# A two-layer streaming encoder on one Trainium2 core: single-group dense turns, residual adds and squares on GpSimd, and two rounds of picks in a step

## The reference, cut to what matters

```
xn  = rmsnorm(x, norm1)                       # x * rsqrt(mean(x*x) + eps) * gain
u   = xn @ w_in                               # one projection, 4292 columns, cut among three mixers
oa  = differential attention (6 heads)        # softmax over two maps, block-causal
ob  = sparse attention (5 heads)              # an indexer scores the keys,
      _, sel = lax.top_k(score, n_sel)        # 256 of them are kept per query (136 for the sample)
oc  = HGRN2 linear recurrence (5 heads)
x   = x + concat(oa', ob, oc') @ w_out
a, gate = split(rmsnorm(x, norm2) @ w_up)     # 2 x 2816 columns
x   = x + (silu(causal_conv3(a)) * gate) @ w_down
```

## Time and profile before

| | us |
|---|---|
| median of 3 runs | 4510.31 (4510.25 to 4512.2) |
| the profiled execution | 4511.78 |
| its span, first to last instruction | 4510.0 |
| TensorE busy | 4080.2 (90%) |
| VectorE busy | 2281.9 (51%) |
| ScalarE busy | 996.6 (22%) |
| GpSimd busy | 224.3 (5%) |
| mean granted TensorE clock | 0.919 of 2.4 GHz |

### The profile page before, as it was taken

How to read it: one execution, slowest core, us unless ns; L and a number is a source line. 1 busy time by engine, 2 the same in 40 slices (tenths; PEclk the granted TensorE clock), 3 DMA queues, 4 the chain that set the end, 5 groups by cost and what they waited for, 6 DMA issues and landing times.

```text
span 4510.0 us, 47853 instructions
## 1 busy us (share of the span) xinstructions
PE 4080.2 (90%) x19244; PEld 2705.0 (60%) x19244; DVE 2281.9 (51%) x4647; ACT 996.6 (22%) x2287; POOL 224.3 (5%) x172
## 2 busy tenths in 40 slices
PE   7888788998889999998999998997899998899998
PEld 6665446776767767773444444486767776644443
DVE  1833454597942454439635555298924555522222
ACT  1113222110113333221223222011123332210001
POOL 2200220000000003100000000400000000000000
PEclk9995788999999999899998989998999998899999
DMA  3321122211120212221221211331121111122222
GB/s 127 109 91 31 53 64 90 77 66 47 52 84 18 69 61 73 87 84 70 70 74 49 73 56 55 108 110 56 45 79 54 47 55 56 37 85 65 77 75 73
DMA packets 142165, 310.33 MB, mean 69 GB/s; under 512 B 29160, under 2 KB 69608, under 8 KB 130680
## 3 DMA queue, kind: packets, MB, share of 16 engines
q1 hardware_dynamic: 81432, 262.25, 17.7%
q10 hardware_dynamic: 60512, 45.02, 3.5%
HBM read 271.08 MB, written 36.14 MB: 68 GB/s over the span
## 4 chain that ended last, share of the span: by engine, by line
PE 73%; DVE 19%; ACT 3%; issue 2%; DMA 1%; ACTq 1%; SPq 0%; DVEq 0%
PE PS L600 49%; PE PS L607 6%; DVE scr L1227 5%; DVE top L1226 5%; PE PS L698 4%; PE PS L687 3%; PE PS L671 3%; PE PS L657 2%; PE PS L576 2%; PE PS L794 1%; PE PS L725 1%; PE PS L793 1%; DVE inv L1164 1%; ACT scr L989 1%; DVE xn L1167 1%
## 5 line engine op out<-in xcount | busy, mean ns | idle before, releaser
L600 PE MATMUL PS<-xn,wring 128*128 128x272 f32 (+1 forms) x6048 | 1906.8, 477 | 74.1 <-DVE xn L1167 48.6
L600 PEld LDWEIGHTS PS<-xn,wring 128*128 128x128 f32 x6048 | 1188.2, 198 | 748.1 <-issue 552.6
L600 PE MATMUL PS<-dense,wring 128*128 128x272 f32 (+1 forms) x2112 | 681.3, 482 | 55.3 <-DVE xT L1173 45.9
L600 PEld LDWEIGHTS PS<-dense,wring 128*128 128x128 f32 x2112 | 417.2, 201 | 288.2 <-issue 217.2
L1173 DVE TENSOR_TENSOR xT<-PS,xT 128x272 f32<-128x272 f32 (+1 forms) x240 | 123.4, 523 | 499.0 <-PE PS L600 497.9
L1226 DVE MAX8 top<-scr 128x8 f32<-128x384 f32 (+6 forms) x418 | 367.5, 879 | 12.7
L1227 DVE MATCH_REPLACE8 scr<-top,scr 128x384 f32<-128x384 f32 (+6 forms) x418 | 359.9, 861 | 0.0
L607 PE MATMUL PS<-wring,xn 128*128 128x224 f32 (+1 forms) x1728 | 350.1, 364 | 10.5 <-ACT dense L865 10.5
L607 PEld LDWEIGHTS PS<-wring,xn 128*128 128x128 f32 (+1 forms) x1728 | 318.0, 187 | 35.5 <-ACT dense L865 11.2
L698 PE MATMUL PS<-kv,scr 128*128 128x64 f32 (+2 forms) x1804 | 249.5, 289 | 14.9 <-ACT scr L989 14.9
L698 PEld LDWEIGHTS PS<-kv,scr 128*128 128x128 f32 (+2 forms) x1804 | 237.6, 202 | 33.8 <-ACT scr L989 21.3
(11 more groups left out here) (160 smaller groups left out, 3090.8 us busy)
## 6 DMA issues: line engine op xcount, KB each, us to landing
wring<-in_wu SPq DMA_DIRECT2D x88, 1024.0 KB, 4.8
wring<-in_wf SPq DMA_DIRECT2D x76, 512.0 KB, 3.3
wring<-in_wd SPq DMA_DIRECT2D x64, 384.0 KB, 3.1
wring<-in_wn SPq DMA_DIRECT2D x24, 896.0 KB, 4.9
wring<-in_wd SPq DMA_DIRECT2D x64, 320.0 KB, 2.9
wring<-in_wo SPq DMA_DIRECT2D x32, 512.0 KB, 3.3
kv<-out_projT ACTq DMA_DIRECT2D x48, 256.0 KB, 4.3
out_projN<-dense SPq DMA_DIRECT2D x96, 112.0 KB, 1.7
```

Source lines behind the costliest of these rows:

```text
L600: mm = nc.tensor.matmul(PS[:, dbank(t.g0 + j), 0:cw], wtile(t.q, i), rhs, start=(kk == a), stop=(kk == b - 1))
```

## The change

- **Turns of one group.** `GRP` of h=1 becomes two groups of 256 columns, and every turn now does a single group j. For f, a, g and the dn of parts 0 to 2 the two groups of a block follow each other; for wo and the last dn all 8 blocks of group 0 come first and then all 8 of group 1 (`_added`), so their weight tiles are loaded twice: 64 more tile loads.
- **Banks of wo and dn are emptied by ScalarE** into one of two buffers `res` (`NRES`), and GpSimd adds that into `xT` (SBUF to SBUF). VectorE's add is gone.
- **Squares of a norm on GpSimd**: in wo turns and in the last dn turns, behind each add, GpSimd squares the block and adds it to a running sum, kept in two blocks of `xn`. The norm's matmul is then one instead of eight, against a matrix of 1/1024 (`mean`). Only the two norms of layer 0's projections still square on ScalarE, into `catT`.
- **Norms by group**: group 0's norm stands behind the third turn of group 1, group 1's behind the first turn of the next stage that uses group 0.
- **Picks**: `BURST = 2`. `weave`'s estimates and leads are adapted; `tout` has two buffers in place of three (`NTO`).
- **Start**: SP loads `mean`, the first half of `xT` (a semaphore per block) and three weight tiles, then the constants and the second half. TensorE waits for `mean` alone.

The core of the diff:

```
-GRP = (((0, 272), (272, 272)), ((0, 512),))
+GRP = (((0, 272), (272, 272)), ((0, 256), (256, 256)))
-BURST = 4
+BURST = 2
...
+def _added(kind, l, h, p, norm):
+    for j in range(2):
+        for n in range(KD):
+            _turn(kind, l, h, n, p, j, load=(kind, l, h, n, p))
+            if (n, j) == (2, 1):
+                _norm(*norm, 0)
 def _ffn(l, h):
-    for n in range(KD):
-        _turn("wo", l, h, n, load=("wo", l, h, n, 0))
-    _norm(l, h, 1)
+    _added("wo", l, h, 0, (l, h, 1))
...
+                order = ("a", 0), ("a", 1), ("g", 0), ("g", 1)
+                for kind, j in (("a", 0), ("g", 0), ("a", 1), ("g", 1)) if n == 0 else order:
+                    _turn(kind, l, h, n, 0, j, load=("u", l, h, n, 0))
+                    if (kind, n, j) == ("a", 0, 0):
+                        _norm(l, h, 1, 1)
...
 dense_scalar:
+                elif t.kind in ("wo", "dn"):
+                    i = ADDS[k]
+                    act.wait_ge(s_res, max(0, i - NRES + 1))
+                    act.wait_ge(s_mm, t.g0 + 1)
+                    nc.scalar.activation(res[:, i % NRES, 0:cw], PS[:, dbank(t.g0), 0:cw], ACT.Copy).then_inc(s_ea, 1)
 dense_vector:
-                elif t.kind in BY_DVE:
-                    for j, (c, cw) in enumerate(GRP[t.h]):
-                        dve.wait_ge(s_mm, t.g0 + j + 1)
-                        x = xT[:, t.n, xcols(t.h, c, cw)]
-                        nc.vector.tensor_tensor(x, PS[:, dbank(t.g0 + j), 0:cw], x, ALU.add).then_inc(s_ed, 1)
 pool_program:
+                if t.kind in ("wo", "dn"):
+                    c, cw = GRP[t.h][t.j]
+                    x, i = xT[:, t.n, xcols(t.h, c, cw)], ADDS[k]
+                    pool.wait_ge(s_ea, t.g0 + 1)
+                    pool.wait_ge(s_xn, KD * norms_before(k))
+                    nc.gpsimd.tensor_tensor(x, x, res[:, i % NRES, 0:cw], ALU.add).then_inc(s_res, 1)
+                    if t.kind == "wo" or t.p == 3:
+                        total, here = xn[:, SUM, c:c + cw], xn[:, SUM + 1, c:c + cw]
+                        pool.wait_ge(s_res, i + 1)
...
+                            own(nc.gpsimd.tensor_tensor(here, x, x, ALU.mult))
+                            ins = nc.gpsimd.tensor_tensor(total, total, here, ALU.add)
...
 sync_program:
+            sp.eng.dma_start(mean[:], io["mean"]).then_inc(s_mean, 16)
             for k in range(KD):
-                sp.eng.dma_start(xT[:, k, :], io["xT"][k * P:(k + 1) * P, :]).then_inc(s_x, 16)
+                sp.eng.dma_start(xT[:, k, 0:W[0]], io["xT"][k * P:(k + 1) * P, 0:W[0]]).then_inc(s_x[0][k], 16)
```

More of the change, by code:

```diff
@@ L282, in weave @@
         l, h = PROJS[m]
-        first = F_TURN[l, h, 5] + 4 if kind == "X" else STAGE["P%d%d" % (l, h)][1] + 3
+        first = LAST["f", l, h, 5, 0] + 1 + LAG if kind == "X" else STAGE["P%d%d" % (l, h)][1] + LAG
         for pe, act, dve, wait in step_times(kind, m):
             steps.append((first, 0.3 + max(wait, act + dve if kind in "CM" else max(act, dve))))
-    turns = [(i, max(0.5, turn_time(TURNS[i])[0])) for i in dense]
+    turns = [(i, turn_time(TURNS[i])) for i in dense]
     have, need = sum(t for i, t in turns), sum(max(0.2, t) for first, t in steps) or 1
@@ L352, in sem @@
             return ctx.enter_context(nc.semaphore(name))
-        ident, ones = sb("ident", [P, P]), sb("ones", [P, P])
+        ident, mean = sb("ident", [P, P]), sb("mean", [P, P])
         lmask, bmask = sb("lmask", [P, NL, 32]), sb("bmask", [P, 4, 32])
@@ L569, in dense_tensor @@
                 if t.kind == "nsq":
-                    N = norm_index(k)
-                    for kk in range(KD):
-                        pe.wait_ge(s_sq, KD * N + kk + 1)
-                        for j, (c, cw) in enumerate(GRP[t.h]):
-                            if kk == 0:
-                                bank_free(pe, t.g0 + j)
-                            mm = nc.tensor.matmul(PS[:, dbank(t.g0 + j), 0:cw], ones[:], sq[:, kk % 2, c:c + cw],
-                                                  start=(kk == 0), stop=(kk == KD - 1))
-                            if kk == KD - 1:
-                                mm.then_inc(s_mm, 1)
-                        if kk < KD - 1:
-                            mm.then_inc(s_sqf, 1)
+                    c, cw = GRP[t.h][t.j]
+                    out = PS[:, dbank(t.g0), 0:cw]
+                    bank_free(pe, t.g0)
+                    if t.p:
+                        for kk in range(KD):
+                            pe.wait_ge(s_sq, KD * norms_before(k) + kk + 1)
+                            mm = nc.tensor.matmul(out, mean[:], catT[:, kk, c:c + cw], start=(kk == 0), stop=(kk == KD - 1))
+                    else:
+                        pe.wait_ge(s_acc, norms_before(k) - 4 + 1)
+                        mm = nc.tensor.matmul(out, mean[:], xn[:, SUM, c:c + cw], start=True, stop=True)
+                    mm.then_inc(s_mm, 1)
                 elif t.kind in ("f", "wo", "a", "g", "dn"):
@@ L635, in idx_tensor @@
                     dots(y, 1)
-                elif what == "pick" and z == 4 and y + 1 < len(PICKS[h]):
+                elif what == "pick" and z == 6 and y + 1 < len(PICKS[h]):
                     dots(y + 1, 0)
@@ L868, in dense_scalar @@
                     U = m * NF + t.n
-                    if t.kind == "a" and t.n == 0:
+                    if t.kind == "a" and t.n == 0 and t.j == 0:
                         for i in range(2):
                             act.wait_ge(s_st[i], max(stored(PROJ_BEFORE[m], r) for r in range(NB) if (PROJ_BEFORE[m] * NB + r) % 2 == i))
-                        for i in range(3):
-                            act.wait_ge(s_to[i], 16 * len([x for x in range(T_COUNT[PROJ_BEFORE[m]]) if x % 3 == i]))
+                        for i in range(NTO):
+                            act.wait_ge(s_to[i], 16 * len([x for x in range(T_COUNT[PROJ_BEFORE[m]]) if x % NTO == i]))
@@ L889, in dense_scalar @@
+                    ins.then_inc(s_ea, 1)
+                    if t.kind == "g" and t.j == 1:
                         pending = (t.l, t.h, t.n, U)
@@ L1151, in dense_vector @@
             for k, t in enumerate(TURNS):
-                if pending is not None and t.kind in ("g", "dn"):
+                if pending is not None and (t.kind == "dn" or k >= LAST[("g",) + pending[0:3] + (0,)] + 2):
                     product()
@@ L1612 @@
         "wd": tiles(a["ffn_down"], P), "rope": np.stack(table(32) + table(64)).transpose(1, 0, 2),
-        "ident": np.eye(P, dtype=np.float32), "ones": np.ones((P, P), np.float32), "lmask": lmask, "bmask": bmask,
+        "ident": np.eye(P, dtype=np.float32), "mean": np.full((P, P), 1.0 / DM, np.float32), "lmask": lmask, "bmask": bmask,
         "fgain": a["final_norm"].reshape(KD, P).T, "clow": clow, "params": params.transpose(1, 0, 2), "lam": lam.transpose(1, 0, 2),
```

284 lines of the change are left out of this document (135 added, 149 removed).

## The result

| | before | after |
|---|---|---|
| median | 4511.26 us (4510.25 to 4514.04, 4 runs) | 4233.31 us (4226.59 to 4238.95, 4 runs) |
| ratio, 95% interval | | 0.9382 (0.9366 to 0.9399) |
| span of the profiled execution | 4510.0 us | 4230.9 us |
| mean granted TensorE clock | 0.919 | 0.944 |
| TensorE busy, not busy | 4080.2, 429.8 us | 3937.3, 293.6 us |

The kernel gained 278 us. So the direction was right, and 148 us, more than half of the gain, were not in the sum.

What follows compares the result with a forecast made beforehand. TensorE, busy 90% of the span, was taken to bound the kernel. The terms -44 - 43 - 42 - 5 - 10 - 20 + 8 + 15 + 12 gave -129, so 4381 us, with a range of 4310 to 4490 us.

Steps and rivals of the forecast that it cites:

- Clock, -20 (0 to -42): F00 and F10 under picks: fewer gaps give back half of the 42 us lost at the lower TensorE clock.
- comes back elsewhere too: Rival: a third of 193 us of clock loss outside P01 and the picks' stretches returns, 64 us; 4317 us, chance 0.14.
- Adds, -44: TensorE's 66.0 us of waits on VectorE's adds into xT go, 22 stay behind ScalarE's copies: -44 us (-66 to -10).
- Norm waits, -43: TensorE's waits on xn and squares, 48.2 us outside the start, are hidden behind turns except 5: -43 us (-48 to -25).
- Norm matmuls, -42: Fewer norm matmuls on TensorE outside first and last norm; those under picks count half: -42 us (-55 to -29).
- Halved groups, +8 (0 to +20): In h=1, a pair of 256-column matmuls costs 0.4313 us in place of 0.4286, 2976 times: +8 us.
- Start, -5: Kernel start: squares start at about 18, first f turn near 28 in place of 36.82: -5 us (+3 to -12).
- End, -10: Behind the last dn turn, 16 us remain in place of 25.8: -10 us (-6 to -12).
- GpSimd, +15: Last dn turns: three GpSimd operations exceed 10 matmuls, 17 us; finished-norm wait taken as covered; +15 us (0 to +54).
- ScalarE, +12: In dn turns ScalarE's copies wait for TensorE where mixers' exponentials could run: 12 waits of 1 us, +12 (0 to +40).
- VectorE does not become the pace: Negates the rival that VectorE stays the pace under picks, late conv and product holding tanh and copies: 4460 us, chance 0.16.
- GpSimd's two cases: Rivals: GpSimd paces wo and last dn turns, 4542 us, chance 0.08; GpSimd waits for VectorE each operation, 4495 us, 0.05.

Runs made afterwards that it cites:

- e2_coarse: The changed kernel with mixer steps allowed only ahead of every second dense turn: 4377.9 us, ratio 0.9703 to the kernel before.
- e4: The changed kernel with both groups' norms in line behind the last wo or dn turn: 4255.8 us, ratio 0.9434 to the kernel before.
- e1: The changed kernel with four rounds of picks in a step in place of two: 4253.2 us, ratio 0.9426 to the kernel before.
- e6: The kernel before with two rounds of picks in a step in place of four, nothing else: 4466.5 us, ratio 0.9906.
- e12: The changed kernel with parameters loaded before the first weight tiles and small computations on constants behind the eighth turn: 4219.2 us, ratio 0.9366 to the kernel before.

## Why the prediction was wrong

By TensorE the 279 us of span are 136 us less idle and 143 us less busy; of the latter 56 are the norms' matmuls that went (85.0 us in the earlier trace rows, 29.2 after), so 87 are, in the main, matmuls that ran faster at the higher level. The sum had 68 of idle (adds 44, norm waits 43, start 5, 3 of the end's 10, less GpSimd's 15 and ScalarE's 12) and 61 of busy (norm matmuls 42 and the end's 7, clock 20, less 8 for halved groups). It missed 68 of idle and 82 of busy, and e2_coarse, which undoes the spacing alone, takes back 70.5 and 71.7.

That these agree so well is in part chance. Along the step-by-step path above, the spacing is worth 146 us where the sum had nothing, and picks, adds and norms' places 150 where it had 87. All the rest together costs 18 us, where the sum had it gaining 42. So 146 and 63 were missed, and 60 were counted too much: 149.

- **The step that failed** is "P01 runs at clock 0.76; its mixers wait on each other there, and the change leaves those alone", with "picks ... nothing". Right is that they wait on each other; wrong is that the change leaves them alone. Turns of one group change how the plan spaces all steps, which undone by itself costs 145 us (e2_coarse), 34 of them in P01. I had priced that part of the change under "halved groups", by its matmuls only. The prediction called itself wrong at its root if P01 changed by over 20 us; it changed by 43.
- **Clock, -20 (0 to -42): mis-sized.** (1 - 0.944) x 4231 = 237 us of span are lost at the lower level against 365, so 128 less. Counting only the two stretches under picks was the error: they gave back 31 of their 42 (clock 0.95 to 1.00 and 0.92 to 0.96), but the time at 1.2 GHz, half of which is lost, also fell from 266 to 205 us in P01, from 120 to 75 in F01, and from 136 to 68 in F10, most of that behind the picks. The rival "comes back elsewhere too" put 64 us outside P01 and the two stretches, and 66 came there; at 4317 it still lacked P01's 31 and all of the waiting.
- **Adds, -44:** undoing them costs 61 us. The wait on ScalarE's copies is 10.5 us where I left 22; at the place of the earlier trace rows 0.76 us stays where 7.8 were forecast, because the conv ahead of the tanh came earlier. The picks halved and the adds moved share one wait, so the two terms cannot be measured apart.
- **Norm waits, -43:** the waits on `xn` left are 14.2 us (under 10 was said). The place of the norms by itself is worth 23 us (e4). **Norm matmuls, -42:** 96 instructions, as said; with the first and last norm, which were counted apart, 56 us went where the terms had 49.
- **Halved groups, +8 (0 to +20):** wrong in the old order, where they cost 40, half of it through the wait on `xT`. With the adds gone from VectorE's order that wait is gone too; what the halving costs in the new order by itself was not tried. The pace held: in F11, with nothing over it, the 1408 matmuls of 256 columns of the a and g turns take 304.8 us, the 704 of 512 before 305.7. The busy share of the weight loads rose from 60 to 76% and cost nothing there.
- **Picks, nothing:** 20 us in the new order (e1), 40 in the old (e6).
- **Start, -5:** the first f turn came at 27.68 us, as said (near 28), but P00 behind it lost it again: P01 begins at 301.9 against 300.5. Behind that turn TensorE waits 20 us in P00 against 15, does the second group's norm matmuls (3.9 us, as said), and its f matmuls take 147.8 us against 144.2. The reason given for the first square, ScalarE behind `s_pre_sum`, holds, and e12 shows some 12 us there. **End, -10:** the tail is 11.5 shorter (14.3 us, 16 said), but F11, said to get 10 shorter, is 2.8 longer, with 7.43 us of waiting for GpSimd ahead of the last norm and 7.5 in place of 3.9 for a wo tile.
- **GpSimd, +15:** the size of an add was right (median 0.757 us), but GpSimd does not pace the last dn turns: in F11 TensorE waits 0.4 us for the copies in all. Its price falls due at the norms, 10.0 us in 2 waits, and 4.31 of that comes from its own wait for a finished norm, which I had called covered. **ScalarE, +12:** TensorE waits 10.5 us for the new copies; its waits for ScalarE's copies of f, t, a and g also grew, from 29 to 52 us, and no run says what of that is this term's.
- **Rivals.** VectorE does not become the pace: under F00's picks it is busy 351.5 of 387.8 us (91%), and TensorE 377.4 (97%). GpSimd's two cases did not come: its adds have a median of 0.757 us, and the last dn turns run at 2.2.

## What to carry to other kernels

When two streams of work share an in-order engine and one of them is a chain across engines, price a change of the other's granularity by the pairs of chain steps that stand together in the merged order: here one whole dense turn (3.8 us) between two steps took away 142 us of waits and slower matmuls, and a plan that lets steps pair up loses them again. Count those pairs in the order before and after before pricing any single instruction. Where steps outnumbered turns, thinning the turns out among them did not pay in the one case tried. And take edits that touch the same waits (adds moved, picks halved, norms moved) together, since undone singly they came to 105 us and together to 150.

## What the runs showed of the hardware

VectorE and GpSimd slow each other where VectorE's two inputs both lie in SBUF. VectorE's product over 512 columns took 691 to 694 ns in all 88 instances before; after, its median is 692 and its longest 1139, and its product over 32 columns takes up to 745 ns against 188. The longest is the one next to the two GpSimd adds at 1008.76 shown above, which took 2.19 us together in place of 1.5:

```profile
1009.19 1.14 DVE L1162 TENSOR_TENSOR dense<-dense 128x512 f32<-128x512 f32 x1
1010.25 0.74 DVE L1164 TENSOR_TENSOR dense<-dense 128x32 f32<-128x32 f32 x1
```

The Trainium skill ("SBUF — State Buffer", Who interferes with whom) says that a VectorE instruction with two SBUF inputs contends with a GpSimd one that reads SBUF, and calls the port pair they share an exclusive lock. The rows agree that both grow where they overlap; they do not show whether one stands still for a whole instruction of the other. They show how little it costs here: the 88 products grew by 2.2 us in all (60.9 to 63.1).

A short wait can have a price beyond itself: right behind 0.58 and 2.00 us of waiting the granted clock fell to 0.50, and the eight score matmuls took 2.93 us in place of 1.56. Not every wait is followed by it: behind the 0.76 us at 1008.82 the clock stayed at 1.00 up to 1025 us. That the loss doubles over the whole span (70.5 us of idle and 71.7 of slower matmuls in e2_coarse) was not expected.
